# Projection order, gate mixing and key products of a two-layer decoder step

## What is computed

```python
def _ab_mixer(x, w_in, vln_g, vln_b, w_s, b_s, sb_bias, w_out, past_k, past_v):
    h = x @ w_in                                   # 1024 -> 5 x 512
    u_a, v_a, q, k, v = jnp.split(h, [W_A, 2 * W_A, 2 * W_A + W_B, 2 * W_A + 2 * W_B], axis=-1)
    u_a = jax.nn.gelu(u_a)
    v_a = _layer_norm(jax.nn.gelu(v_a), vln_g, vln_b)
    a_out = _chunk_gmlp(u_a, v_a, w_s, b_s)        # u * (tril(w) mixed over chunks of 128 rows + b)
    ...                                            # stick-breaking attention of q, k, v, 8 heads of 64
    y = jnp.concatenate([a_out, b_out.reshape(B, T, W_B)], axis=-1) @ w_out
    return y, k, v, v_a

def _sb_weights(z, causal):
    log_keep = jnp.where(causal, -jax.nn.softplus(z), 0.0)
    shifted = jnp.concatenate([log_keep[..., 1:], jnp.zeros_like(log_keep[..., :1])], axis=-1)
    suffix = lax.cumsum(shifted, axis=3, reverse=True)
    return jnp.where(causal, jnp.exp(jax.nn.log_sigmoid(z) + suffix), 0.0)
```

## Time and profile before

| what | us |
|---|---|
| median of three runs | 1903.36 |
| lowest and highest | 1900.83, 1906.38 |
| the profiled execution | 1903.15 |
| its span | 1901.1 |

### The profile page before, as it was taken

How to read it: one execution, slowest core, us unless ns; L and a number is a source line. 1 busy time by engine, 2 the same in 40 slices (tenths; PEclk the granted TensorE clock), 3 DMA queues, 4 the chain that set the end, 5 groups by cost and what they waited for, 6 DMA issues and landing times.

```text
span 1901.1 us, 33407 instructions
## 1 busy us (share of the span) xinstructions
PE 1796.4 (94%) x12706; PEld 1566.5 (82%) x12706; DVE 885.2 (47%) x1410; ACT 523.9 (28%) x739; POOL 143.2 (8%) x119
## 2 busy tenths in 40 slices
PE   8999899988999999979989989989987999999996
PEld 7676444688999999978859949949946899999995
DVE  3123666347553355444263264254256655245544
ACT  3122344123221222133222322322233322122213
POOL 0000000002000000006013012011110100000000
PEclk9999899998999999999999999999998999999999
DMA  7876477421222222212333333323323222222321
GB/s 273 290 251 239 171 253 246 176 68 56 87 88 93 76 88 92 94 57 79 117 133 108 130 127 105 139 110 110 123 115 99 71 86 93 87 78 88 97 96 47
DMA packets 84070, 234.40 MB, mean 123 GB/s; under 512 B 9633, under 2 KB 9794, under 8 KB 83506
## 3 DMA queue, kind: packets, MB, share of 16 engines
q1 hardware_dynamic: 83138, 228.26, 35.9%
q0 software_dynamic: 880, 5.49, 0.8%
HBM read 209.90 MB, written 23.80 MB: 123 GB/s over the span
## 4 chain that ended last, share of the span: by engine, by line
PE 87%; DVE 6%; DMA 3%; ACT 2%; issue 2%; SPq 1%; DVEq 0%; ACTq 0%
PE banks L1236 69%; PE banks L1266 3%; PE banks L1361 2%; PE banks L1443 2%; PE banks L1525 2%; PE banks L1517 1%; PE banks L1400 1%; PE banks L1387 1%; DMA w_raw<-in_w_in_ab 1%; PE banks L1415 1%; PE banks L1505 1%; DVE x_lo L1009 1%; DMA s<-in_s 1%; DVE y L988 1%; SPq L294 1%
## 5 line engine op out<-in xcount | busy, mean ns | idle before, releaser
L1236 PE MATMUL banks<-x_hi,w_hi 128*128 128x272 f32 x2624 | 549.6, 291 | 37.2 <-DVE x_lo L1009 28.2
L1236 PE MATMUL banks<-x_hi,w_lo 128*128 128x272 f32 x2624 | 545.9, 290 | 0.0
L660 DVE TENSOR_TENSOR w_lo<-w_raw,w_hi 128x1024 fp32r<-128x1024 f32 (+2 forms) x228 | 277.5, 1217 | 572.8 <-ACT w_hi L438 572.6
L1236 PE MATMUL banks<-x_lo,w_hi 128*128 128x272 f32 x2624 | 543.9, 289 | 0.0
L438 ACT ACTIVATE w_hi<-w_raw 128x1024 fp32r<-128x1024 f32 (+2 forms) x228 | 238.4, 1046 | 1085.1 <-PE banks L1236 910.9
L1236 PEld LDWEIGHTS banks<-x_hi,w_hi 128*128 128x128 f32 x2624 | 414.6, 189 | 55.4 <-issue 34.4
L1236 PEld LDWEIGHTS banks<-x_lo,w_hi 128*128 128x128 f32 x2624 | 415.2, 190 | 0.0
L1236 PEld LDWEIGHTS banks<-x_hi,w_lo 128*128 128x128 f32 x2624 | 412.6, 190 | 0.0
L1236 PE MATMUL banks<-act_hi,w_lo 128*128 128x272 f32 x704 | 145.3, 287 | 0.0
L1236 PE MATMUL banks<-act_lo,w_hi 128*128 128x272 f32 x704 | 145.1, 287 | 0.0
L1236 PE MATMUL banks<-act_hi,w_hi 128*128 128x272 f32 x704 | 145.1, 287 | 0.0
(11 more groups left out here) (228 smaller groups left out, 1696.4 us busy)
## 6 DMA issues: line engine op xcount, KB each, us to landing
w_raw<-in_w_up SPq DMA_DIRECT2D x88, 512.0 KB, 3.5
kv<-in_kc SPq DMA_DIRECT2D x128, 256.0 KB, 4.2
kv<-in_vc SPq DMA_DIRECT2D x128, 256.0 KB, 4.2
w_raw<-in_w_rin SPq DMA_DIRECT2D x48, 512.0 KB, 3.5
w_raw<-in_w_dn SPq DMA_DIRECT2D x32, 704.0 KB, 4.0
s<-in_s SPq DMA_DIRECT2D x32, 512.0 KB, 7.3
out_ret_s<-s SPq DMA_DIRECT2D x32, 512.0 KB, 2.7
w_raw<-in_w_in_ab SPq DMA_DIRECT2D x20, 512.0 KB, 6.1
```

The source lines that it names most:

```text
L660: V.tensor_tensor(w_lo[:, j, 0:k * P], w_raw[:, j, 0:k * P], w_hi[:, j, 0:k * P].bitcast(F32), ALU.subtract).then_inc(lo_ready, 1)
L1236: last = mm(B[:, 2 * j + half, 0:HN], a[:, j, w], x[:, kt, half * HN:(half + 1) * HN], start=kt == 0 and n == 0, stop=kt == k - 1 and n == 2)
```

## The change

- The weight tiles come in the order q, k, the gate's v, the gate's u, v. With it `natural(0, ...)` moves one step forward, to steps 11 to 13, and `natural(4, ...)` behind the loop, between the scores of heads 0 and 1, through banks 3 and 5.
- Gate mixing moves from behind the loop to steps 17 (samples and two pairs) and 18 (two pairs), all through banks 5 and 6; VectorE adds and multiplies the samples at once (`mix_samples`) and the blocks in two operations each. The norm of the gate's v takes two fused passes where it took three.
- A half sample of keys fills all four column groups with 256 columns each; the page table is laid out for it. `qk(15)` moves behind `pr_qk(0)`.
- `pr_qk(n)` waits for `pr_z(n - 1)`, `pr_qk(1)` moves ahead of the turns; `av` takes the column groups in the order 1, 2, 3, 0.
- Of ScalarE's four table loads in and behind the projection loop two are left, both behind tile 15; the logarithm of the new keys comes after them, `new_zr` and the triangle's product in step 16.
- The first two output tiles are loaded between the last pages of values, and split in turns 6 and 7; the store of v comes behind the projection.

```diff
-GM_BANK = [5, 6, 3, 4]
+GM_BANK = [5, 6, 5, 6]
+V_BANK = [3, 5]
...
-            for i in range(2):
-                load(A["w_out_ab"], i, U_OUT_AB + i, i, KD)
-                load_half(N_IN_AB - 4 + i)
-            for q in range(N_IN_AB - 2, 4 * DEC_B):
+            for q in range(N_IN_AB - 4, 4 * DEC_B):
                 load_half(q)
+                if q >= 4 * DEC_B - 6 and q % 2:
+                    i = (q - (4 * DEC_B - 5)) // 2
+                    if i < 2:
+                        load(A["w_out_ab"], i, U_OUT_AB + i, i, KD)
...
             def evict_in(u):
-                split(u + 2, u % 2, KD)
+                if u + 2 < N_IN_AB:
+                    split(u + 2, u % 2, KD)
+                else:
+                    act.wait_ge(tile_done, u + 1)
...
             for u in range(12):
                 evict_in(u)
-            nc.scalar.preload_act_table_set("natural_log_exp_and_others")
+            copy_va(0, 2)
             evict_in(12)
-            copy_va(0, 2)
+            copy_va(2, 4)
             evict_in(13)
-            copy_va(2, 4)
-            log_part(zn[:, :, :, :].rearrange(flat), lnn[:, :, :, :].rearrange(flat), zn_ready, 1, lnn_ready)
+            copy_va(4, NB + 1)
             evict_in(14)
-            copy_va(4, NB + 1)
             evict_in(15)
-            act.wait_ge(znr_ready, 1)
-            nc.scalar.activation(an[:, :, :, :].rearrange("p b c h -> p c b h"), zn[:, :, :, :], ACT.Exp)\
-                .then_inc(an_ready, 1)
             nc.scalar.preload_act_table_set("sqrt_and_others")
             act.wait_ge(first_in, 2 * 16)
             act.wait_ge(va_var, 1)
             nc.scalar.activation(vrs[:, :], vmv[:, :, 1], ACT.Sqrt, bias=eps).then_inc(va_std, 1)
-            nc.scalar.preload_act_table_set("gelu_apprx_tanh_and_others")
-            for u in range(16, N_IN_AB):
-                evict_in(u)
             nc.scalar.preload_act_table_set("natural_log_exp_and_others")
+            log_part(zn[:, :, :, :].rearrange(flat), lnn[:, :, :, :].rearrange(flat), zn_ready, 1, lnn_ready)
+            evict_in(16)
+            evict_in(17)
+            act.wait_ge(znr_ready, 1)
...
             act.wait_ge(va_ready, NB + 1)
             dec_log(0)
+            evict_in(18)
+            evict_in(19)
+            act.wait_ge(tile_done, U_IN_AB + N_IN_AB)
             for pr in range(4):
                 act.wait_ge(gm_out, pr + 1)
                 copy(x_hi[:, pr, :], uT[:, pr, :]).then_inc(gm_hi, 1)
+            dec_exp(0)
             pr_log(0)
-            dec_exp(0)
             dec_log(1)
...
+                else:
+                    split(U_OUT_AB + n + 2 - DEC_B, n % 2, KD)
...
+                if u == 16:
+                    new_zr()
                 if u >= 6 and u % 2 == 0:
                     dec_z((u - 6) // 2)
...
+                if u == 15:
+                    new_sp()
+                    va_gain()
                 if u == 16:
                     va_shift()
...
-            for pr in range(4):
-                mix_gate(pr)
+            mix_samples()
+            mix_gate(0)
+            mix_gate(1)
+            dec_z(6)
+            mix_gate(2)
+            mix_gate(3)
...
             dec_sp(0)
-            pr_z(0)
             for pr in range(4):
                 dve.wait_ge(gm_hi, pr + 1)
...
             dec_zr(0)
+            pr_z(0)
+            z_rows(DEC_B - 1)
+            copy_v(0, 2)
             dec_z(DEC_B - 1)
+            copy_v(2, 4)
             pr_sp(0)
             dve.wait_ge(z_ready, 2)
             dec_sp(1)
+            copy_v(4, NB + 1)
...
+                else:
+                    low(U_OUT_AB + n + 2 - DEC_B, n % 2, KD)
...
+                h = q % 2 * 256
                 for c in range(4):
-                    for r in range(first // 2, (first + HALF) // 2):
-                        last = mm(B[32 * r:32 * r + 32, 4, :], qz[:, b, c, :],
-                                  view(kv[:, 2 * r, 0, :], (512, 4), (1, P), off=c * P), start=c == 0, stop=c == 3)
+                    for r in range(4):
+                        last = mm(B[32 * r:32 * r + 32, 4, h:h + 256], qz[:, b, c, :],
+                                  view(kv[:, first + r, 0, :], (512, PER_SLOT), (1, P), off=c * P),
+                                  start=c == 0, stop=c == 3)
...
+                if u == 16:
+
+                    pe.wait_ge(spn_ready, 1)
...
+                if u == 17:
+                    gate_samples()
+                    gate_blocks(0)
+                    gate_blocks(1)
...
+                if 4 <= u < N_IN_AB - 1:
+                    qk(u - 4)
+                if u == 16:
+                    pe.wait_ge(znr_ready, 1)
+                    z_columns(5)
+                if u == 11:
+                    for j in range(2):
+                        pe.wait_ge(evicted[j], (U_IN_AB + 12) // 2 + 1)
+                if 11 <= u < 14:
+                    t = (u - 11) * 2
+                    natural(0, t, min(t + 2, NB + 1), cop_a, nat_a, (5, 6))
+                if u == 18:
+                    gate_blocks(2)
+                    gate_blocks(3)
...
-                for s in range(first, first + HALF):
-                    pe.wait_ge(kv_landed[s], 32 * (DEC_B + b) + 32)
-                    for g in range(PER_SLOT):
-                        k, r = divmod(PER_SLOT * s + g, 4)
-                        last = mm(B[32 * r:32 * r + 32, 7, :], ad[:, b % 2, :, 4 * r + k], kv[:, s, g, :],
+                for g in range(PER_SLOT):
+                    for r in (1, 2, 3, 0):
+                        pe.wait_ge(kv_landed[first + r], 32 * (DEC_B + b) + 32)
+                        k = PER_SLOT * (q % 2) + g
+                        last = mm(B[32 * r:32 * r + 32, 7, :], ad[:, b % 2, :, 4 * k + r], kv[:, first + r, g, :],
                                   start=k == 0 and r > 0, stop=k == 3)
...
+            pe.wait_ge(gm_taken, 4)
+            suffix(0)
+            for j in range(2):
+                pe.wait_ge(evicted[j], (U_IN_AB + N_IN_AB) // 2 + 1)
             pr_qk(0)
-            pe.wait_ge(gm_out, 4)
+            qk(2 * DEC_B - 1)
+            natural(4, 0, 2, cop_b, nat_b, V_BANK)
+            pr_qk(1)
             z_columns(DEC_B - 1)
-            suffix(0)
+            natural(4, 2, 4, cop_b, nat_b, V_BANK)
             pe.wait_ge(an_ready, 1)
             pe.wait_ge(z_ready, DEC_B)
             for n in range(H_B):
-                if n + 1 < H_B:
+                if 0 < n < H_B - 1:
                     pr_qk(n + 1)
+                if n == 0:
+                    natural(4, 4, NB + 1, cop_b, nat_b, V_BANK)
+                    pe.wait_ge(cop_b, NB + 1)
                 av(2 * n)
```

More of the change, by code:

```diff
@@ L714, in va_variance, with va_gain, va_shift @@
                 last.then_inc(va_var, 1)
-            def va_centred():
+            def va_gain():
+                dve.wait_ge(mix_in, 5 * 16)
+                dve.wait_ge(va_var, 1)
+                for t in range(NB + 1):
+                    rows = rows_of_block(t)
+                    step.add(V.scalar_tensor_tensor(va_nat[0:rows, t, :], va_nat[0:rows, t, :], vmv[0:rows, t, 0:1],
+                                                    vlng[0:rows, :], ALU.subtract, ALU.mult))
+            def va_shift():
                 dve.wait_ge(va_std, 1)
@@ L775, in new_zr @@
                     .then_inc(znr_ready, 1)
-            for u in range(N_IN_AB):
+            for u in range(N_IN_AB - 2):
                 low(u + 2, u % 2, KD)
@@ L795, in _, with mix_samples @@
                     step.add(V.tensor_scalar(lnp[:, :, 0, :], lnp[:, :, 0, :], -0.5, None, ALU.mult))
+                if u == 12:
+                    va_stats(0, 2)
                 if u == 13:
                     new_z()
[L798 removed]
+                    va_stats(2, 4)
                 if u == 14:
[L800 to L802 removed]
                     va_stats(4, NB + 1)
                     va_variance()
[L805 removed]
+                if u == 15:
+                    new_sp()
+                    va_gain()
                 if u == 16:
[L807 to L814 removed]
+                    va_shift()
+            def mix_samples():
+                dve.wait_ge(gm_mixed, 1)
+                dve.wait_ge(mix_in, 5 * 16)
+                gm = gmix[:, 0:4 * TS].rearrange("p (a n) -> p a n", a=4)
+                for pr in range(4):
+                    last = V.tensor_tensor(gm[:, pr, :].rearrange("p (b t) -> p b t", t=DEC_T),
+                                           B[:, 7, pr * TS:(pr + 1) * TS].rearrange("p (b t) -> p b t", t=DEC_T),
+                                           view(brep[:, pr, :], (0, DEC_B), (1, DEC_T)), ALU.add)
+                    last.then_inc(gms_taken, 1)
+                dve.wait_ge(gms_taken, 4)
+                for j in range(2):
+                    dve.wait_ge(evicted[j], (U_IN_AB + 16) // 2 + 1)
+                step.add(V.tensor_tensor(uT[:, :, TP:NT], gm, uT[:, :, TP:NT], ALU.mult))
+                step.wait()
             def mix_gate(pr):
```

(21 more changed lines are left out.)

104 lines of the change are left out of this document (24 added, 80 removed).

## The result

| what | before | after |
|---|---|---|
| median, us | 1904.87 (4 runs, 1900.83 to 1906.60) | 1880.30 (4 runs, 1879.82 to 1883.05) |
| ratio | | 0.9881, 95% interval 0.9863 to 0.9898 |
| the profiled execution, its span | 1903.15, 1901.1 | 1879.82, 1877.7 |

The changed kernel is 1.2% faster. Forecast were 1878 us and a range of 1866 to 1892. The windows of the changed kernel by stage show where the 23.4 us of span went: projection from the first half sample of keys to the end of tile 19, passage to the first product of the turns, then the turns (from:to, length, busy us and instructions of PE, PEld, DVE, ACT, POOL, clock, DMA share, GB/s).

The account below looks back on a forecast made before the run. TensorE was taken to bound the projection and the attention turns, with a low-clock passage between. Terms -24.8 - 7.7 + 5.5 + 9.4 + 2.5 - 10.2 = -25.3 took 1903.15 to 1878 us, range 1866 to 1892.

Parts of the forecast that it names:

- Keys: Half samples in the projection: four column groups cut each from 3.56 to 1.90 us, -24.8 us over fifteen.
- Rival 3: Projection's keys: 256-column products of four groups do not overlap, a half takes 6.8 us, 1940 us in all; chance 0.05.
- rival 2: Projection's keys: weight loads are not hidden, a half takes 3.0 us, 1889 us in all; chance 0.06.
- rival 1: Projection: a step cannot go below its transfers' 9.65 us, so keys give only 4.5 us, 1892 us in all; chance 0.08.
- Wait for v, transposes, gate mixing: Projection: step 17's wait for v goes and twenty transposes leave, -7.7 us; mixing enters steps 17 and 18, +5.5 us.
- New waits: Projection steps 10, 11 and 16: PE waits on chains that do not shrink as the steps do, +9.4 us.
- Clock: Projection: PE runs at a lower clock after the waits at steps 11 and 16, +2.5 us (0 to 5).
- Projection: First layer's mixer projection, bound by TensorE: tile 19 was to end some 15 us earlier.
- Passage: From tile 19's end to the turns' first product: 27.6 becomes 17.4 us, -10.2 us (-6 to -13).
- Turns: Eight turns of attention: no net change, 0 us (-6 to +6), depending on where low-clock spells fall.
- The sum: Whole kernel: all terms together -25.3 us, from 1903.15 to 1877.9, said as 1878 us.

Follow-up runs that it names:

- all four moves: Changed kernel with gate's v transposes one step later, new keys' logarithm before the root, last v copy earlier, kT stored behind the projection: 1863.0 us, ratio 0.9783.
- the second profile: The changed kernel itself, unedited, run and profiled once more on the same chip: 1878.9 us, ratio 0.9854 to the kernel before.

## Why the prediction was right, point by point

- **Keys.** Right, and for the reason given. A half takes 1.87 us, 1.90 was forecast, so 15 x 1.69 = 25.4 us instead of 24.8. Alone the keys give 22 us (by the ratio) to 24 (by the medians). Rival 3 (no overlap, 6.8 us) and rival 2 (loads visible, 3.0 us) are out by the half itself, rival 2 also by the 64 loads.
- **Transfers (rival 1).** Out as a floor of the step: the steps at the full clock take 49.26 - 41.19 = 8.07 us, where 8.1 was forecast and the rival had some 9.5. With all four moves the DMA share rises to 0.87 and the projection still runs at TensorE's pace.
- **Wait for v, transposes, gate mixing.** Right: no wait for v in the projection, and the samples and two times two pairs take 0.6 and twice 2.5 us, waiting for nothing.
- **New waits.** The sum was right, 9.5 against 9.4 us; all four places were named. That the store of kT makes `z_rows` late at step 10 is shown: with the store moved the wait is gone. How the waits of step 16 divide was not: 3.0 and 0.8 us against 1.8 and 2.4. The split of tile 17 started 11.0 us after the half ahead of it (138.63 to 149.67) where I had carried over 9.9 from step 12 before. SP took 4.65 us to issue the eight pages ahead of that tile, where the row that I used has 3.94, which is 0.7 of the 1.1 us; its queue in the changed kernel, three steps in a row:

```profile
130.07 3.94 SPq L296 DMA_DIRECT2D kv<-in_kc  x8
134.05 0.43 SPq L263 DMA_DIRECT2D w_raw<-in_w_in_ab  x1
138.91 4.65 SPq L296 DMA_DIRECT2D kv<-in_kc  x8
143.61 0.43 SPq L263 DMA_DIRECT2D w_raw<-in_w_in_ab  x1
147.31 4.90 SPq L296 DMA_DIRECT2D kv<-in_kc  x8
```

  And `new_zr` was less late because PE, at the low clock, came to it later: its half took 3.64 us. In the kernel with 128 columns, where that half ran at the full clock (1.95 us), the two waits are 2.3 and 3.0 us, in the proportion of the forecast.
- **Clock.** This is the term that was mis-sized. I put +2.5 us (0 to 5) behind the waits, from one stretch of 3.4 us behind one wait; the profiled execution paid 8.6, outside the bounds, and "over 10 us" of low clock in the projection, named as what would make the prediction wrong, came true with 20.5. In the second profile the same order had 10.2 and paid 4.7, inside the bounds. So the term was too small, and its bounds too narrow for one of the two executions. It also left a place out: no price was put on the clock behind step 10, and the 3.4 us there cost 1.7 in the first profile and nothing in the second.
- **Projection.** Tile 19 ends at 191.82, 9.8 us earlier, where -15.1 was forecast. The clock took 6.1 us more than forecast and the quicker halves gave 0.6 back, which accounts for the 5.3 us that are missing to within 0.3. In the second profile the projection is 14.4 us shorter.
- **Passage.** Right in size and in detail: 17.0 us against 17.4 (PE waits 4.76 us for the copy, where 5 to 6 was forecast), set by the last copy of v behind `pr_sp(0)` and `dec_sp(1)`. The timeline of VectorE in the changed kernel has the chain of the forecast:

```profile
202.66 1.28 DVE L745 COPY v_nat<-banks 128x512 f32<-128x512 f32 x2
203.86 1.48 DVE L898 SCALAR_TENSOR_TENSOR lp<-zp,lp 128x1280 f32<-128x1280 f32 x1
...
206.11 0.68 DVE L849 SCALAR_TENSOR_TENSOR sp<-z_low,ld 128x512 f32<-128x512 f32 x1
...
206.93 1.29 DVE L854 TENSOR_TENSOR_SCAN inc<-smask,sp 128x544 f32<-128x544 f32 x1
208.14 0.65 DVE L745 COPY v_nat<-banks 32x512 f32<-32x512 f32 x1
```

- **Turns.** 0 was forecast (-6 to +6), -3.2 came, by the clock, and in another execution with the same turns -0.2. That the order of the groups is worth nothing was right.
- **The sum.** -25.3 forecast, -23.3 in the profiled executions: 5.3 too much from the projection, 0.4 too little from the passage and 3.2 from the turns. Two errors by the clock, of opposite sign, cancelled in part; that the time came closer than its terms is luck. Turn 0 started 20.4 us earlier, where some 25 was forecast. Small slips in the working change nothing: 3.65 + 0.75 + 1.1 is 5.5 and not 5.4, 0.65 + 2 x 2.5 is 5.65 and not 5.5, and z_rows at step 10 comes out 1.7 late and not 1.5.

## What to carry to other kernels

Cost a step that gets shorter together with the chains that do not: here the landing of the next tile and the eviction behind it kept their length, and 9.5 us of waits with 8.6 us of low clock, where 3.6 and 1.7 stood before, took back half of what the keys gave. Look for such waits in the order of the queues before giving up the gain; four moves of order, with no work taken out, won another 16 us. Give a term that hangs on the clock a wide bound, for the same order of work paid 8.6 us in one execution and 4.7 in the next.

## What the runs showed of the hardware

- Products that alternate over four column groups ran four at a time down to 128 columns: a half takes 1.87 us as 16 products of 256 and 1.88 as 32 of 128, with all rows used by each and 32 or 64 weight loads hidden. In two blocks of two groups a half takes 2.75 us, and products start out of the order in which they stand: the second block's first pass starts at 50.59, ahead of the first block's last at 51.22.
- The low stretches differ in length behind the same waits: 20.5, 10.2, and with another order of the values' groups 17.1 us, for 8.7 to 9.8 us of idle time. With 2.3 us of idle time there was none. In the turns, where PE hardly waits (0.6 to 1.9 us), 17 to 25 us of low clock remain in every kernel. Where PE waits 4.76 us ahead of turn 0, the first of these stretches starts within that wait; where it waits 0.77 us there is none at that place, but 17.1 us still come later. No run here shows what sets those off, and that stays open.
- SP's issue of eight pages took between 3.94 and 5.80 us in one execution, and so moved the tile that stands behind them in the queue. In the issue of 4.65 us, for one, a single page took 1.05 us where the others took 0.33.
